# Attention scores in three short-format multiplications of high and low parts in place of one in full width

## The reference

```python
q = rope((x @ w_q).reshape(B, S, N_BRANCHES * N_HEADS, HEAD_DIM), positions)
...
s = jnp.einsum("brhnqd,brhnkd->brhnqk", qb, kk).astype(jnp.float32)
...
s = jnp.where(mask, s, NEG_INF)
```

## Time and profile before

| | |
|---|---|
| three timed runs | 1116.19, 1116.43, 1117.71 us; median 1116.43 |
| profiled execution | 1117.65 us, span of the trace 1115.6 us |
| mean granted clock of PE | 0.998 |
| PE busy | 1100.5 us, 99% |
| DVE busy | 755.4 us, 68% |
| attention steps 1 to 8, first to last score block | 328.3 to 557 us, one each 33 us |

### The profile page before, as it was taken

How to read it: one execution, slowest core, us unless ns; L and a number is a source line. 1 busy time by engine, 2 the same in 40 slices (tenths; PEclk the granted TensorE clock), 3 DMA queues, 4 the chain that set the end, 5 groups by cost and what they waited for, 6 DMA issues and landing times.

```text
span 1115.6 us, 18330 instructions
## 1 busy us (share of the span) xinstructions
PE 1100.5 (99%) x6820; PEld 998.2 (89%) x6820; DVE 755.4 (68%) x1161; ACT 593.3 (53%) x871; POOL 54.6 (5%) x47
## 2 busy tenths in 40 slices
PE   7999999999999999999999999999999999999998
PEld 6997888888999999999978888888999989999987
DVE  6976755564686676766657555655777687989970
ACT  6436654453645555553567454644446656656640
POOL 0100000000000000000000000000020011122210
PEclk9999999999999999999999999999999999999999
DMA  8554756666495545452246656682626564655670
GB/s 275 187 179 154 245 169 199 234 216 199 130 230 157 164 130 152 125 157 75 95 122 190 203 172 223 212 262 59 199 83 200 159 220 124 188 180 188 227 245 19
DMA packets 215670, 193.75 MB, mean 174 GB/s; under 512 B 9609, under 2 KB 190909, under 8 KB 215613
## 3 DMA queue, kind: packets, MB, share of 16 engines
q1 hardware_dynamic: 215401, 192.88, 55.7%
q10 hardware_dynamic: 212, 0.09, 0.0%
HBM read 191.88 MB, written 1.05 MB: 173 GB/s over the span
## 4 chain that ended last, share of the span: by engine, by line
PE 96%; DVE 1%; ACT 1%; DMA 1%; SPq 0%; issue 0%; DVEq 0%; ACTq 0%
PE ps L665 14%; PE ps L667 14%; PE ps L666 14%; PE ps L610 8%; PE ps L611 8%; PE ps L612 8%; PE ps L764 6%; PE ps L766 6%; PE ps L765 6%; PE ps L819 2%; PE ps L845 2%; PE ps L834 1%; PE ps L853 1%; PE ps L679 1%; PE ps L713 1%; PE ps L677 1%
## 5 line engine op out<-in xcount | busy, mean ns | idle before, releaser
L1643 DVE TENSOR_TENSOR w_lo<-raw,w_hi 128x1024 fp32r<-128x1024 f32 (+1 forms) x298 | 398.6, 1382 | 57.2 <-ACT w_hi L1207 56.8
L1207 ACT ACTIVATE w_hi<-raw 128x1024 fp32r<-128x1024 f32 (+1 forms) x298 | 331.1, 1156 | 123.8 <-PE ps L667 34.1
L610 PE MATMUL ps<-x_hi,w_hi 128*128 128x256 f32 x656 | 186.7, 285 | 0.0
L612 PE MATMUL ps<-x_hi,w_lo 128*128 128x256 f32 x656 | 185.6, 283 | 0.0
L611 PE MATMUL ps<-x_lo,w_hi 128*128 128x256 f32 x656 | 185.6, 283 | 0.0
L665 PE MATMUL ps<-w_hi,x_hi 128*128 128x512 f32 (+1 forms) x328 | 129.1, 394 | 0.0
L667 PE MATMUL ps<-w_hi,x_lo 128*128 128x512 f32 (+1 forms) x328 | 127.5, 389 | 0.0
L666 PE MATMUL ps<-w_lo,x_hi 128*128 128x512 f32 (+1 forms) x328 | 127.3, 388 | 0.0
L610 PEld LDWEIGHTS ps<-x_hi,w_hi 128*128 128x128 f32 x656 | 125.8, 192 | 1.3 <-issue 1.3
L611 PEld LDWEIGHTS ps<-x_lo,w_hi 128*128 128x128 f32 x656 | 125.9, 192 | 0.0
L612 PEld LDWEIGHTS ps<-x_hi,w_lo 128*128 128x128 f32 x656 | 125.8, 192 | 0.0
(11 more groups left out here) (231 smaller groups left out, 1779.0 us busy)
## 6 DMA issues: line engine op xcount, KB each, us to landing
raw<-in_ffn_w_gate_up SPq DMA_DIRECT2D x176, 256.0 KB, 4.2
raw<-in_w_up SPq DMA_DIRECT2D x44, 512.0 KB, 4.5
raw<-in_ffn_w_down SPq DMA_DIRECT2D x24, 768.0 KB, 5.9
raw<-in_conv_w_in SPq DMA_DIRECT2D x24, 512.0 KB, 5.0
raw<-in_w_q SPq DMA_DIRECT2D x48, 256.0 KB, 4.3
raw<-in_w_kv SPq DMA_DIRECT2D x48, 256.0 KB, 4.3
raw_v<-in_w_kv SPq DMA_DIRECT2D x48, 256.0 KB, 4.2
raw<-in_w_in SPq DMA_DIRECT2D x20, 512.0 KB, 4.5
```

The costliest lines, as they stand in the source:

```text
L610: nc.tensor.matmul(o, wh[:, k0 + k, c], hi[:, k, :], start=(k == 0), stop=False)
L612: ins = nc.tensor.matmul(o, wl[:, k0 + k, c], hi[:, k, :], start=False, stop=(k == kt - 1))
L1207: nc.scalar.activation(w_hi[:, s, a * ph.cols:b * ph.cols], src, ACT.Copy)\
L1643: nc.vector.tensor_tensor(w_lo[:, s, c], src, w_hi[:, s, c], ALU.subtract)\
```

## The change

qT and kT become float32r. DVE makes qT_lo and kT_lo with four new subtractions a step, low(0) to low(3), from the same PSUM banks less the stored high parts, into the idle slot of w_lo; each waits for its qk_stored and adds 1 to a new semaphore, qk_low. PE waits for qk_low wherever it waited for qk_stored. Each of the 12 score multiplications becomes three of the short format, terms 0 to 2: high queries and high keys, low queries and high keys, high queries and low keys. S_ORDER is computed: for each head the entries follow one another with a running count of 128-column units, and the 36 entries of both heads are sorted by that count. Head 0 does its three narrow ones (query tile 0) first, head 1 its wide ones. On DVE, low(n) is put in between the other work, and split_next(1) is cut in two around low(2).

```diff
--- before.py
+++ after.py
@@ -158,8 +158,10 @@
 
         e = a_at
         m_hi = at("m_hi", [P, KD, T], F32R, e)
-        kT = at("kT", [P, 3, T], F32, e + 8192)
-        qT = at("qT", [P, 3, T], F32, e + 11264)
+        kT = at("kT", [P, 3, T], F32R, e + 8192)
+        qT = at("qT", [P, 3, T], F32R, e + 11264)
+        kT_lo = at("kT_lo", [P, 3, T], F32R, names["w_lo"][0] + SLOT * 4)
+        qT_lo = at("qT_lo", [P, 3, T], F32R, names["w_lo"][0] + SLOT * 4 + 3072)
         v_tok = at("v_tok", [P, 2, 3 * P], F32, e + 14336)
         rope_a = at("rope_a", [P, 2, 3 * P], F32, e + 17408)
         m_lo = at("m_lo", [P, KD, T], F32R, e + 22528)
@@ -315,6 +317,7 @@
         prob_stored = sem("prob_stored")
         head_done = sem("head_done")
         o_stored = sem("o_stored")
+        qk_low = sem("qk_low")
         o_hi, o_split = sem("o_hi"), sem("o_split")
         qk_squared, qk_summed, qk_rooted = sem("qk_squared"), sem("qk_summed"), sem("qk_rooted")
         windowed, pooled = sem("windowed"), sem("pooled")
@@ -489,8 +492,16 @@
         N_CONST = 16 * (sum(len(g) for g in VECS[1:]) + 3)
         TILE_BANK, TILE_BANK_0 = (0, 1, 2, 0, 1, 2), (0, 1, 2, 3, 4, 5)
         S_AT = ((3 * 512, 5 * 512), (4 * 512, 6 * 512 + 256))
-        S_ORDER = ((0, 0, 0), (1, 1, 0), (0, 0, 1), (0, 0, 2), (1, 0, 0), (0, 1, 0), (1, 0, 1), (1, 0, 2), (0, 1, 1),
-                   (1, 1, 1), (0, 1, 2), (1, 1, 2))
+        S_PLACES = ([(0, 0, g) for g in range(3)] + [(0, 1, g) for g in range(3)],
+                    [(1, 1, g) for g in range(3)] + [(1, 0, g) for g in range(3)])
+        S_ORDER = []
+        for places in S_PLACES:
+            units = 0
+            for hh, qt, g in places:
+                for term in range(3):
+                    S_ORDER.append((units, hh, qt, g, term))
+                    units += qt + 1
+        S_ORDER.sort()
         PT_AT = ((384, 0), (1152, 1920))
         TURNS = 4 * 8
         HEADS, PAIRS = 16, 8
@@ -810,17 +821,18 @@
                         pe.wait_ge(v_stored, 1)
                     else:
                         pe.wait_ge(o_stored, q)
-                    pe.wait_ge(qk_stored, q * 4 + 4)
-                    for hh, qt, g in S_ORDER:
+                    pe.wait_ge(qk_low, q * 4 + 4)
+                    for _, hh, qt, g, term in S_ORDER:
                         w, f = P * (qt + 1), slice(hh * HD, (hh + 1) * HD)
                         o0 = S_AT[hh][qt] + g * w
-                        if (hh, qt, g) == (0, 1, 2):
+                        if (hh, qt, g, term) == (0, 1, 2, 0):
                             pe.wait_ge(bank_scored, q + 1)
-                        ins = nc.tensor.matmul(flat[:, o0:o0 + w], qT[f, g, tok(qt)], kT[f, g, 0:w], start=True, stop=True,
-                                               skip_group_check=True)
-                        if (hh, qt, g) == (1, 1, 0):
+                        q_, k_ = (qT_lo if term == 1 else qT), (kT_lo if term == 2 else kT)
+                        ins = nc.tensor.matmul(flat[:, o0:o0 + w], q_[f, g, tok(qt)], k_[f, g, 0:w], start=(term == 0),
+                                               stop=(term == 2), skip_group_check=True)
+                        if (hh, qt, g, term) == (1, 1, 0, 2):
                             ins.then_inc(bank_scored, 1)
-                        if (qt, g) == (1, 2):
+                        if (hh, qt, g, term) in ((0, 1, 2, 2), (1, 0, 2, 2)):
                             ins.then_inc(scored, 1)
 
                 def turn_p():
@@ -892,7 +904,7 @@
                     value()
                 else:
                     ready(ph, 0, i, bank=False)
-                    pe.wait_ge(qk_stored, i * 4)
+                    pe.wait_ge(qk_low, i * 4)
                     token_major(ph, 0, 0, banks[0], m_hi, m_lo, signal=1, done=tile_a_done)
                     score()
                     pe.wait_ge(va_stored, i)
@@ -903,15 +915,15 @@
                     token_major(ph, 1, 0, banks[2], x_hi, x_lo, signal=1, done=tile_a_done)
                     turn_p()
                     turn(1)
-                    pe.wait_ge(qk_stored, i * 4 + 1)
+                    pe.wait_ge(qk_low, i * 4 + 1)
                     token_major(ph, 1, 1, banks[3], x_hi, x_lo, signal=1)
                     value()
                     turn(2)
                     ready(ph, 2, i, bank=False)
-                    pe.wait_ge(qk_stored, i * 4 + 2)
+                    pe.wait_ge(qk_low, i * 4 + 2)
                     token_major(ph, 2, 0, banks[4], x_hi, x_lo, signal=1, done=tile_a_done)
                     turn(3)
-                    pe.wait_ge(qk_stored, i * 4 + 3)
+                    pe.wait_ge(qk_low, i * 4 + 3)
                     token_major(ph, 2, 1, banks[5], x_hi, x_lo, signal=2)
 
             def hybrid_turn(r):
@@ -1889,11 +1901,11 @@
                     c = hh * 1152
                     normalise(prob[:, c:c + 1152], (slice(0, 384), slice(384, 1152)), q * 2 + hh, SOFT2[hh])
 
-                def split_next(j):
+                def split_next(j, parts=(0, 1)):
                     if last:
-                        split(*next_chunk(ph, ph.count + j))
+                        split(*next_chunk(ph, ph.count + j), parts=parts)
                     else:
-                        split(ph, j, i + 1)
+                        split(ph, j, i + 1, parts=parts)
 
                 def store_v(t):
                     if t == 0:
@@ -1902,6 +1914,12 @@
                         dve.wait_ge(product_done, ph.n(3, i) + 1)
                     nc.vector.tensor_scalar(v_tok[:, t, :], ps[:, banks[4 + t], 0:384], rcol[:, t:t + 1], None, ALU.mult)\
                         .then_inc(v_stored if t else va_stored, 1)
+
+                def low(n):
+                    dve.wait_ge(qk_stored, i * 4 + (n + 1))
+                    hi, lo = (qT, qT_lo) if n < 2 else (kT, kT_lo)
+                    nc.vector.tensor_tensor(lo[:, :, tok(n % 2)], ps[:, banks[n], 0:384].rearrange("p (g c) -> p g c", g=3),
+                                            hi[:, :, tok(n % 2)], ALU.subtract).then_inc(qk_low, 1)
 
                 if not project:
                     split(w_o_, 2, 0, parts=(0,))
@@ -1920,7 +1938,11 @@
                     split(ph, 2, i)
                     for n in range(1, 4):
                         rope(i, n, banks)
+                        if n > 1:
+                            low(n - 2)
                     split_next(0)
+                    low(2)
+                    low(3)
                     store_v(0)
                     store_v(1)
                     split_next(1)
@@ -1932,13 +1954,18 @@
                     scale(0)
                     rope(i, 1, banks)
                     scale(1)
+                    low(0)
                     split_next(0)
                     rope(i, 2, banks)
                     if last:
                         output_low(0, 6)
+                    low(1)
                     rope(i, 3, banks)
-                    split_next(1)
+                    split_next(1, parts=(0,))
+                    low(2)
+                    split_next(1, parts=(1,))
                     store_v(0)
+                    low(3)
                     if last:
                         output_low(6, 7)
                     store_v(1)
```

## The result

| | before | changed |
|---|---|---|
| median of 6 runs | 1116.35 us (1115.93 to 1117.71) | 1121.89 us (1120.91 to 1123.39) |
| profiled execution | 1117.65 us, span 1115.6 | 1121.21 us, span 1119.1 |

The changed kernel is slower by 0.5%: ratio 1.0047, 95% interval 1.0035 to 1.006. The forecast was 1121.0 us, in a range of 1116.4 to 1124.5, and slower by more than 0.2%. In the median it is 5.5 us more, in the profiled executions 3.6.

What follows compares the result with a forecast made beforehand. The prediction took TensorE (PE), busy for 99% of the span, as the bound. Score blocks +1.6 us, first step +1.8 and clock nothing, added to the profiled 1117.65 us, gave 1121.05, in a range of 1116.4 to 1124.5.

Steps and rivals of the forecast that it cites:

- The block: Score block of each head pair: +0.2 us a pair for short-format multiplications, 8 x 0.2 = +1.6 us.
- the price at free running: Score block: 2.30 us against 2.16 if the heads run freely side by side, +0.14 us a pair.
- the order: Score block: listing a wide multiplication as two narrow ones; strictly kept, 2.77 us, +0.6 a pair; taken near the free end.
- The first step: Pause before attention step 1: PE waits for all four DVE low parts of step 0, +1.8 us, range 1.5 to 2.4.
- The hidden low parts: Steady attention steps: 4 x 0.48 = 1.9 us of DVE work a step hidden by PE's projections, no new wait.
- The clock: After the pause before step 1: a half-clock stretch costing 1.5 us, expected in every run; nothing against the profiled run.
- a possible further loss: Half-clock stretch after the pause before step 1: it may last longer, a loss of up to 1.7 us.
- A: Score block: narrow short-format multiplications don't pay the 0.107 us load; -1.6 us there, total 1117.9 us; chance 0.16.
- B: Score block: the halves don't run side by side in the short format; +17 us there, total 1136.5 us; chance 0.08.
- C: Score block: narrow short-format multiplications run at the full width's rate; +9.3 us there, total 1128.7 us; chance 0.05.

Runs made afterwards that it cites:

- x8: Changed kernel with the two heads' multiplications strictly in turn and narrow ones moving 256 columns instead of 128; 1122.16 us, one run.
- x4: Changed kernel with the list of score multiplications alternating strictly between the two heads; 1120.45 us, ratio 1.0031.
- x2: Changed kernel with scores multiplied in full width as before; DVE's low parts and their waits kept, results unused; 1120.05 us, ratio 1.0029.
- x6: Changed kernel with split_next(0) before rope(2) in step 0 and step 1's first wait for one low part only; 1118.18 us, ratio 1.0011.
- x5: Kernel before, full width, with split_next(0) before rope(2) in step 0 and step 1 first waiting for one store only; 1114.27 us, ratio 0.9978.
- x1: Changed kernel without DVE's low parts: all three terms multiply high parts and PE waits for qk_stored; 1119.29 us, ratio 1.0022.
- x7: Changed kernel with split_next(0) moved early, step 1 first waiting for one low part, and heads strictly in turn; 1116.47 us, ratio 1.0002.
- x9: Changed kernel with all 18 score multiplications of head 1 listed ahead of all 18 of head 0; 1139.92 us, one run.

## Why the prediction was right

**The block.** Forecast +0.2 us a pair, measured +0.22. The step that carried it is the load of 0.107 us read from the first multiplication behind the block; the narrow one came at 0.11 us as said, and x8 confirms that columns are not its price. The order was rightly placed between free and strict, near the free end, but the two parts were not weighed right: the forecast took 0.14 for the price at free running and 0.06 for the order, and x4 gives 0.09 and 0.13. That the total came within 0.02 us is luck in so far as the two errors go opposite ways.

**The first step.** Forecast +1.8, measured 1.79: four low parts at 0.46 to 0.47 us, 0.48 forecast, one of them partly in the gap between two ropes. The forecast put the gap at 0.1 where the rows give 0.17, and that made up for a handover to PE 0.1 us longer than before.

**The hidden low parts.** Right for the changed kernel: x2's steady steps have the length they had. x6 shows the limit of it. The slack in step 1 held only because PE was late by the same amount.

**The clock.** That a stretch would come in every execution, and that the median of the kernel before is one without, was right and carried 1.2 of the 4.6 us over the median; without it the forecast would have been 1119.8. x2 and x5 show both ends: none of six executions at mean clock 1.0 with the pause of 3.6 us, all of eleven with none before step 1. What failed is the reason given for a possible further loss, that the stretch might last longer. It kept its length, 3.4 us in every profile. The further loss of some 1.5 us in half of the executions is, by x8, most likely a second stretch, behind a pause at 17 us that the prediction never looked at. The three at 0.998 have their median at 1121.21, 0.2 us over the forecast, so this is most of the 0.9 us by which the median of all six lies over it. That the share of executions with the early stretch would be the same in both kernels was not measured.

**The rivals.** A (loads free) would have given a block under 2.1 us, B and C over 3. The two halves run side by side in the short format too: 36 multiplications of 0.11 to 0.12 us in 2.26 us.

**The working.** Three of its sums are off, and none decides the result. The ends that it gives for block, first step and clock add up to 1119.7 and 1126.5 us, so the range of 1116.4 to 1124.5 isn't what it is said to be made of; the measured 1121.9 lies inside both. The lowest of those ends is 0.3% above the median, so no corner of the forecast lies within 0.2% of it, where 0.06 was put. And rival B is 4.18 - 1.95 = 2.2 us a pair, not 2.1.

## What to carry to other kernels

Splitting a full-width multiplication into three short-format ones trades two instructions for three, so it pays only where the moving side is wide enough to hide each one's weight load: here at 256 columns, 3 x 0.12 against 2 x 0.216, and not at 128 columns, 3 x 0.112 against 2 x 0.109. By these prices a head with only its wide ones in the short format would take 6 x 0.109 + 9 x 0.12 = 1.73 us against 1.95; that is an estimate, and such a kernel was not run. When two half arrays run side by side, list their work in turn by the measured time of each piece and not by its columns. Before optimizing a busy engine's work, look at its pauses: moving one DVE instruction pair into idle time, with the wait that goes with it, brought 2.3 us, while every short form of the scores tried here was slower than the full width with the same placing of DVE's split (x1 against before, x6 and x7 against x5).

## What the runs showed of the hardware that I had not expected

A short-format multiplication of 128 columns on 64 rows takes 0.111 us in a stream, hardly less than one of 256 columns with 0.12; behind wide ones the first narrow one took 0.06 (x9). Half-array multiplications passed up to three listed ahead of them for the other half, and no more (x9 and the changed kernel). The Trainium skill, page "TensorE: Matmul & The Clock Gate", section "The mechanism", has multiplications in strict program order; x9 and the earlier trace rows disagree with it. In x9 the clock also fell to 1.2 GHz without any pause, behind score blocks of 3.95 us in each of which one head's multiplications ran alone for the first 1.69 us:

```profile
441.80:445.00 3.20, 3.20 (x12) 3.20 (x11) 3.09 (x12) 1.77 (x5) 0.00 (x0) 0.50 0.54 159
```

The block ended at 441.41. It happened behind three of eight such blocks and behind none of 2.17 to 2.57 us. What in these blocks brings it was not tested by itself.
